# The first weight tile of an encoder kernel, issued from ScalarE's DMA queue instead of between the halves of x on SyncE's

## What is computed

```python
for l in range(DEPTH):
    h = rms_norm(x, ffn1_norm_pre[l])
    h = swiglu(h, ffn1_w_gate[l], ffn1_w_up[l], ffn1_w_down[l])   # silu(h @ w_gate) * (h @ w_up) @ w_down
    x = x + 0.5 * rms_norm(h, ffn1_norm_post[l])
    ...
```

## Time and profile before

| | |
|---|---|
| median of 3 runs | 956.77 us (955.39 to 956.92) |
| the profiled execution | 956.9 us, of which the span from the first to the last instruction is 955.1 us |
| PE busy | 943.0 us, 99% of the span |
| DVE, ACT, POOL busy | 676.0, 527.1, 25.1 us |
| mean granted TensorE clock | 0.999 of full speed |
| DMA | 180.29 MB, mean 189 GB/s |

### The profile page before, as it was taken

One profiled execution on the slowest core, in us unless ns is written; L12 is line 12 of the kernel. 1 busy time (PEld: TensorE's weight loads), 2 busy tenths in 40 slices (PEclk: granted clock), 3 DMA queues, 4 the chain that ended last, 5 costly groups with the idle time before them and its releaser, 6 DMA issues.

```text
span 955.1 us, 12878 instructions
## 1 busy us (share of the span) xinstructions
PE 943.0 (99%) x5185; PEld 814.7 (85%) x5185; DVE 676.0 (71%) x986; ACT 527.1 (55%) x699; POOL 25.1 (3%) x44
## 2 busy tenths in 40 slices
PE   8999999999999999999999999999999999999997
PEld 7888888888987888888888888888889888888886
DVE  6966867787788856656688666657878877665654
ACT  6645544558776545445565444445697565544542
POOL 0300000000000012000000000000000000000000
PEclk9999999999999999999999999999999999999999
DMA  9688556457424767655466656556554366565641
GB/s 308 209 258 289 176 193 204 132 192 236 147 89 141 263 214 202 200 194 181 153 205 220 211 179 205 190 178 196 192 184 132 108 201 199 191 205 178 188 165 45
DMA packets 131914, 180.29 MB, mean 189 GB/s; under 512 B 4120, under 2 KB 115368, under 8 KB 131856
## 3 DMA queue, kind: packets, MB, share of 16 engines
q1 hardware_dynamic: 129504, 175.65, 56.4%
q0 software_dynamic: 2192, 3.76, 1.9%
q10 hardware_dynamic: 160, 0.07, 0.0%
HBM read 178.40 MB, written 2.63 MB: 190 GB/s over the span
## 4 chain that ended last, share of the span: by engine, by line
PE 88%; DVE 7%; ACT 2%; issue 1%; DMA 1%; DVEq 0%
PE UP L435 31%; PE Y L462 24%; PE UP L440 16%; PE UP L733 4%; PE Y L450 3%; PE UP L738 2%; DVE wlo L1147 1%; PE UP L746 1%; PE Y L494 1%; PE Y L496 1%; PE Y L500 1%; ACT junk L852 1%; PE UP L474 1%; DVE xs L1211 1%; DVE logit L1432 1%
## 5 line engine op out<-in xcount | busy, mean ns | idle before, releaser
L1147 DVE TENSOR_TENSOR wlo<-raw,whi 128x2048 fp32r<-128x2048 f32 x152 | 347.9, 2291 | 125.4 <-ACT whi L835 125.4
L835 ACT ACTIVATE whi<-raw 128x2048 fp32r<-128x2048 f32 x159 | 304.0, 1913 | 96.8 <-DMA raw<-in_ffn_w_gate 72.3
L435 PE MATMUL UP<-xT,whi 128*128 128x512 f32 x1280 | 304.8, 390 | 0.0
L435 PEld LDWEIGHTS UP<-xT,whi 128*128 128x128 f32 x1280 | 237.4, 188 | 47.5
L462 PE MATMUL Y<-whi,yT 128*128 128x512 f32 x736 | 206.5, 391 | 0.0
L440 PEld LDWEIGHTS UP<-xT,wlo 128*128 128x128 f32 x1280 | 164.1, 191 | 6.2
L440 PE MATMUL UP<-xT,wlo 128*128 128x256 f32 x1280 | 166.0, 283 | 0.0
L462 PEld LDWEIGHTS Y<-whi,yT 128*128 128x128 f32 x736 | 135.2, 188 | 25.6
L462 PE MATMUL Y<-wlo,yT 128*128 128x512 f32 x368 | 113.7, 390 | 0.0
L937 ACT ACTIVATE gate_small<-UP 128x512 f32<-128x512 f32 x40 | 23.8, 595 | 106.8 <-PE UP L440 106.5
L462 PEld LDWEIGHTS Y<-wlo,yT 128*128 128x128 f32 x368 | 69.1, 188 | 14.8
(11 more groups left out here) (219 smaller groups left out, 878.2 us busy)
## 6 DMA issues: line engine op xcount, KB each, us to landing
raw<-in_ffn_w_up SPq DMA_DIRECT2D x44, 1024.0 KB, 5.3
raw<-in_ffn_w_down SPq DMA_DIRECT2D x44, 1024.0 KB, 5.0
raw<-in_ffn_w_gate SPq DMA_DIRECT2D x43, 1024.0 KB, 5.3
raw<-in_w_in SPq DMA_DIRECT2D x20, 1024.0 KB, 5.3
raw<-in_w_out SPq DMA_DIRECT2D x8, 1024.0 KB, 5.0
gains<-in_ffn_norm_post SPq DMA_DIRECT2D x4, 512.0 KB, 6.6
shift_scratch<-shift_rows POOLq DMA_DIRECT2D x1, 1536.0 KB, 12.5
gains<-in_ffn_norm_pre SPq DMA_DIRECT2D x3, 512.0 KB, 5.9
```

Source lines behind the costliest of these rows:

```text
L435: nc.tensor.matmul(bank(UP, b + c), h[:, kt, c * P:c * P + P], xT[:, kt, :, :].rearrange("p h s -> p (h s)"), start=kt == 0, stop=False, s ...
L835: A.activation(whi[:, k % RING, :], raw[:, k % RING, :], ACT.Copy).then_inc(hi_ready, 1)
L1147: V.tensor_tensor(wlo[:, k % RING, :], raw[:, k % RING, :], whi[:, k % RING, :].bitcast(F32), ALU.subtract).then_inc(lo_ready, 1)
```

## The change

Both halves of unit 0 leave SP's program and stand in ACT's: the first between the gain and `ident`, the second behind `ident`, ahead of the load of the square root's table. SP issues the four quarters of x one behind the other and then unit 1. On PE `keep_clock(3)` becomes `keep_clock(1)`. (In ACT's part a helper's line numbers differ between the listings; the operations are the same.)

```diff
@@ sync
             load_x(0)
-            load_first(0)
             load_x(1)
-            load_first(1)
             load_cols(1, a["ffn1_w_up"], 0, 0)
@@ tensor, enter_first
                 turn(0, 0, 0)
                 turn(0, 0, 1)
-                keep_clock(3)
+                keep_clock(1)
                 first_unit(0, 0, 0)
@@ scalar (load_first is defined here now, with act.dma_start for sp.dma_start)
+            def load_first(h):
+                act.dma_start(cols(0, raw)[:, 4 * h:4 * h + 4, :],
+                              a["ffn1_w_gate"][0, HALF * h:HALF * h + HALF, 0:UC].rearrange("(k p) n -> p k n", p=P)).then_inc(raw_loaded[0] if h else first_loaded, 16)
+
             act.dma_start(gain_rows, a["ffn1_norm_pre"][0:1, :].rearrange("a (k p) -> (a k) p", p=P)).then_inc(gain_loaded, 16)
+            load_first(0)
             act.dma_start(ident[:, :], consts["ident"][:, :]).then_inc(ident_loaded, 16)
+            load_first(1)
             load_root_table()
```

More of the change, by code:

```diff
@@ L342, in load_x @@
                     sp.dma_start(x[:, t, feature_half(h)], a["x"][0, t * P:(t + 1) * P, feature_half(h)]).then_inc(x_loaded[t][h], 16)
-            def load_first(h):
-                sp.dma_start(cols(0, raw)[:, 4 * h:4 * h + 4, :],
-                             a["ffn1_w_gate"][0, HALF * h:HALF * h + HALF, 0:UC].rearrange("(k p) n -> p k n", p=P)).then_inc(raw_loaded[0] if h else first_loaded, 16)
             load_x(0)
-            load_first(0)
             load_x(1)
-            load_first(1)
             load_cols(1, a["ffn1_w_up"], 0, 0)
```

## The result

The changed kernel takes **960.86 us** (median of 6 runs, 960.58 to 961.52) against 956.85 us before; the ratio is 1.0045, 95% interval 1.0035 to 1.0055. It is slower by about 4 us, more than twice the 1.8 us forecast, and the time lies just above the range given. (One of the six runs of before, at 2425 us, was a disturbed one and is left out of the ratio.) The profiled execution has a span of 958.8 us, 3.7 above the 955.1 of before, so the sum of this document is made against 3.7.

The account below looks back on a forecast made before the run. PE bounds the kernel, so only its continuous start counts: ident's landing 8.3 + 5.85 = 14.15 against 12.35, +1.8 us, 958.6 us. The likeliest case's range was 957.4 to 960.0, the 8-in-10 range 956.0 to 960.7.

Parts of the forecast that it names:

- What bounds the kernel, and that only the start matters: PE, busy 99% of the span: whatever moves its continuous start, 12.35 us, moves the end by the same amount.
- That ident, behind the half tile, becomes what PE waits for: ACT's queue delivers in order, so ident lands no earlier than the 512 KB ahead, and PE's transposes wait for it.
- The chain of I + 5.85: From ident's landing I through transposes, copies and products, PE is continuous 5.85 us later; break-even at I = 6.5.
- the rounded weights: At the first products: landed ahead of ident, needing 1.06 us on ACT, ready first by about a microsecond.
- I = 8.3: Ident's landing at the start, taken as 8.3 us from two queues sharing the DMA engines evenly; before, 4.7.
- the upper bound of 9.7: Ident's landing if descriptors of x and the weights took turns one by one; the sum is then +3.2 us.
- The row: DMA from 66 to 70 us: q1 moved 0.58 MB and q0 0.63 MB, taken to show even sharing by bytes.
- That the clock stays up: In PE's wait for ident the forecast kept the clock up, adding nothing to +1.8 us; this case had 0.54.
- The slow clock: Rival, chance 0.22: the clock falls in PE's 3.5 us wait for ident, 1.2 to 2.0 on top, +3.0 to +3.8.
- keep_clock(1), the second half tile, ACT's two more issues at 0: At the start, three parts put at 0: fewer multiplications in a wait, loads needed after 10 us, issues needed later.
- That the weights gain nothing: First half of unit 0 on ACT's queue: its advance is no more than the 0.3 us of earlier issue.

Follow-up runs that it names:

- ident last: The changed kernel with ident issued behind both halves of unit 0 in ACT's queue: 963.44 us, ratio 1.0072.
- 26 multiplications: The changed kernel with 26 multiplications of ones instead of 8 ahead of the wait for ident: 959.84 us, ratio 1.0031.
- the second profile: The changed kernel run again with nothing altered, as mate of two later kernels: 960.79 us, ratio 1.0043 to the kernel before.
- the one with 20 multiplications: The changed kernel with 20 multiplications of ones instead of 8 ahead of the wait for ident: 959.22 us, ratio 1.0033.
- ident on SP: The changed kernel with ident issued by SP between x's first two quarters, not in ACT's queue: 959.4 us, ratio 1.0027.
- keep_clock alone: The kernel before with keep_clock(1) for keep_clock(3) and nothing else: 956.92 us, ratio 0.9997.

## Why the prediction was wrong, step by step

**What bounds the kernel, and that only the start matters: right.** Every kernel of the study moves the span by what it moves the bias product, within 0.3 us: 20.60 - 16.89 = 3.71 for a span 3.7 longer in the changed one.

**That ident, behind the half tile, becomes what PE waits for: right.** The wait of 4.42 us at L531 is it; ident last makes it 8.50 us and the time 6.6 us longer.

**The chain of I + 5.85: right within 0.2 us, at the full clock.** 5.87 and 5.82 us were measured where the clock was held, but from the gain's transpose, which starts 0.1 to 0.2 us behind the landing. One premise of it was wrong without harm: the rounded weights are not ready a microsecond ahead. ACT's program has the root ahead of the rounding, the root waits for DVE's `base_sum`, and that stands behind `gain_cols`, which needs `ident`. So the rounding starts at 10.07 in the changed kernel, 1.9 us behind the landing of the half tile, and is done at 11.11, still ahead of xT at 12.34; with 26 multiplications the margin was 0.3 us (11.15 and 11.46). It is a second path from `ident` to the products.

**I = 8.3: too early; it was 9.1.** This term of the sum was off by 0.8 us. It has the half tile about right (8.2) and `ident` directly with it; `ident` came 0.9 us behind. In four profiles of this order `ident` landed between 7.9 and 9.3, 0.1 to 0.9 us behind the half tile, which is scatter that the one value did not show; the upper bound of 9.7 covered it. Two readings under the term were weak. The row is of a hardware queue beside POOL's software queue, not of two hardware queues, and the sharing that it shows began only near 5 us; by then q10 had moved 0.34 MB beside 0.53 of q1. And a landing is not the moment at which as many bytes have been moved: in the kernel before q1 had moved 1.04 MB by 6.0 us, as much as x's first half and the half tile together, yet the half tile landed at 8.3, and by 8.0 q1 had moved 1.66 MB. So bytes of later loads were moved ahead of its last ones. Why the last ones come so late was not measured.

**That the clock stays up: this step failed.** The slow clock was the rival with 0.22, at +3.0 to +3.8, and it is what happened: +3.7 in the profile, 4.0 in the runs. In the second profile it fell in the wait, as the rival has it; in the first it was low behind the wait, and may never have been up. Its price was put at 1.2 to 2.0 and measured at 0.9 in one profile (6.79 against 5.87), 1.7 in the other (7.55 against 5.85), 1.6 between the medians of the changed kernel and the one with 20 multiplications, though that holds some scatter of the landing too. What misled was to place 3.5 us of idleness by its length alone, between the harmless 2.17 and the 4.7 of the kernel's end. The harmless gap stood behind the whole opening, in which PE had worked until 7.2; in the changed kernel the gap follows eight multiplications alone. With 2.40 us of gap behind those eight the clock fell, with 1.62 behind those, two more and the transposes of one quarter of x (ident on SP) it fell too, and with 2.14 behind the full opening (keep_clock alone) it did not. The end of the kernel is no row for this: it says how late the fall came after the longest work, not how early it can come.

**The sum for the changed kernel's profile**, then: 1.8 as forecast, 0.8 for I, 0.9 for the clock, and 0.2 by which the chain behind the landing was short. That is 3.7, the whole.

**keep_clock(1), the second half tile, ACT's two more issues at 0: right** for the first, shown alone (0.9997); for the others nothing in the chain points to them.

**That the weights gain nothing: borne out as far as it was run.** With x's second half out of its way the second queue gives 956.78 us, the time of before. That agrees with the Trainium skill's "DMA: Bandwidth & Descriptors", section "Issuing engines are not separate DMA queues", by which only issuing time is saved. Its section "Queues, rings and completion order" has each DMA engine switch between the rings of two queues packet by packet. The rows from 4.8 us on agree (0.18 beside 0.19 MB). Those from 4.1 to 4.8 do not show it: q1 moved 0.01 MB beside 0.19 of q10, with a load of q1 issued since 1.66. Why it had nothing to move there was not measured; that whatever prepares the packets takes the loads in the order of issue would fit both stretches, and is argued only.

## What to carry to other kernels

A small load on which everything waits (an identity, a gain) belongs ahead of the large ones of its queue. A second hardware queue is no way around the first: near the start of this kernel, what was issued first over both queues began to move first, and from then on the two shared. Where a wait is moved to a place at which PE has done little, count the clock into its price: about two idle microseconds that cost nothing behind the full opening cost one to two behind eight multiplications. And ask of a filler how long it lasts against the wait that it covers: 12 more multiplications of ones ahead of `ident` won 1.6 us, and two fewer behind the transposes lost nothing. Last, give a landing that a sum rests on a range and not one value: the same load in the same order landed anywhere between 7.9 and 9.3.

## What the hardware showed beyond that

- A half tile issued 0.1 us behind a quarter of x on the other queue (1.77 against 1.66) landed at 10.5, against 8.2 where it was issued 0.3 us ahead of that quarter and 7.9 where that quarter and all behind it were held back. From 4 to 5 us it moved 0.02 MB, in the last case 0.16.
- Of two loads in flight the one issued later can land first: x's third quarter at 7.7 (issued at 1.66, 256 KB), the half tile at 8.2 (issued at 1.36, 512 KB), on two queues.
- The granted clock fell to 1.2 GHz around idle stretches of 2.40 us behind eight multiplications and of 1.62 us behind little more, and held over 2.17 and 2.14 us where PE had worked until about 7 us. Once down it stayed there through as much as 6 us of nearly unbroken work (9.4 to 15.4 us in the second profile of the changed kernel).
